# Second attention reordered with its attended product in halves, expert requests reordered, unread products in the waits of the router: one change to a two-layer trunk with experts

## What is computed

```python
def neighborhood_attention(h_lat, h_ctx, w_qkv, w_o, rpb, ctx_out):      # layer 1, 16 heads of 64
    ...
    s_loc = einsum(q_r, k_blk) + bias                                    # bias is -1e30 outside the window
    s_ctx = einsum(q_r, kc)
    p = softmax(concatenate([s_loc, s_ctx], -1))
    o = einsum(p[..., :n_loc], v_blk) + einsum(p[..., n_loc:], vc)
    ...
    return o @ w_o

def moe_ffn(h, router_w, router_bias, w_gate, w_up, w_down):
    scores = sigmoid(h @ router_w); sel = scores + router_bias
    # the best of 4 groups, the best 2 experts in it; gates from their scores
    for e in range(16):
        y = y + gates[:, e:e+1] * ((silu(h @ w_gate[e]) * (h @ w_up[e])) @ w_down[e])
```

## Time and profile before

| what | value |
|---|---|
| median of 3 runs | 1212.77 us (1210.61 to 1214.37) |
| the profiled execution | 1215.52 us |
| its span, first to last instruction | 1213.4 us |
| mean granted TensorE clock | 0.905 |
| PE, DVE, ACT, POOL busy | 79%, 33%, 31%, 18% of the span |
| layer 0: router and experts | about 405 to 676 us |
| attention of layer 1 | about 828 to 907 us |
| layer 1: router and experts | about 942 to 1185 us |

### The profile page before, as it was taken

One profiled execution on the slowest core, in us unless ns is written; L12 is line 12 of the kernel. 1 busy time (PEld: TensorE's weight loads), 2 busy tenths in 40 slices (PEclk: granted clock), 3 DMA queues, 4 the chain that ended last, 5 costly groups with the idle time before them and its releaser, 6 DMA issues.

```text
span 1213.4 us, 24157 instructions
## 1 busy us (share of the span) xinstructions
PE 957.7 (79%) x9458; PEld 638.5 (53%) x9459; DVE 402.5 (33%) x809; ACT 372.5 (31%) x803; POOL 218.3 (18%) x329
## 2 busy tenths in 40 slices
PE   3699999978799488897998389997889279876540
PEld 0477776535455344564766268885445147653320
DVE  1433330557623512121221562224543612221103
ACT  3533222557511222121222453235432112221102
POOL 0000000000000044343443105700000233442211
PEclk8899999999899689898999789999889589998875
DMA  9766655996401839999997574317037769999972
GB/s 342 255 230 230 213 208 208 319 388 233 194 14 44 338 108 413 422 422 425 422 423 298 185 199 114 139 60 287 1 89 302 286 260 420 421 423 423 425 323 110
DMA packets 93681, 322.05 MB, mean 265 GB/s; under 512 B 21241, under 2 KB 33954, under 8 KB 81330
## 3 DMA queue, kind: packets, MB, share of 16 engines
q1 hardware_dynamic: 85746, 305.40, 65.1%
q0 software_dynamic: 7008, 12.62, 2.8%
q10 hardware_dynamic: 864, 3.15, 0.6%
HBM read 313.67 MB, written 13.99 MB: 270 GB/s over the span
## 4 chain that ended last, share of the span: by engine, by line
PE 58%; DMA 24%; DVE 8%; SPq 4%; issue 3%; ACT 3%; POOL 1%; DVEq 0%; POOLq 0%; ACTq 0%
PE ps L1641 20%; PE ps L1859 19%; DMA expert_sets<-in_moe_w_up_dram 17%; PE ps L1783 7%; PE ps L1544 3%; DMA ada_late<-in_ada_w_dram 3%; PE ps L1568 2%; PE ps L1747 2%; DMA ring<-in_diff_w_qkv_dram 2%; SPq L608 1%; PE ps L1694 1%; SPq L590 1%; DMA expert_rows<-moe,scatter_idx 1%; DVE att L1312 1%; DMA val<-expert_rows 1%
## 5 line engine op out<-in xcount | busy, mean ns | idle before, releaser
L1859 PE MATMUL ps<-expert_sets,moe 128*32 128x256 f32 x6304 | 370.2, 397 | 98.5 <-DMA expert_sets<-in_moe_w_up_dram 67.8
L1859 PEld LDWEIGHTS ps<-expert_sets,moe 128*32 128x32 f32 x6304 | 243.2, 115 | 224.1 <-issue 123.4
L1502 DVE STREAM_TRANSPOSE moe<-moe 128x256 f32<-128x256 f32 x70 | 45.9, 655 | 326.9 <-PE ps L1859 305.7
L1641 PE MATMUL ps<-w_high,x_high 128*128 128x512 f32 x352 | 141.8, 403 | 6.1 <-DVE hT L506 2.7
L1641 PE MATMUL ps<-w_high,x_low 128*128 128x512 f32 x352 | 138.9, 394 | 0.0
L1641 PE MATMUL ps<-w_low,x_high 128*128 128x512 f32 x352 | 138.4, 393 | 0.0
L1066 ACT ACTIVATE moe<-ps 128x128 f32<-128x128 f32 x68 | 18.9, 278 | 273.8 <-PE ps L1859 271.6
L741 POOL MEMSET moe<- 128x128 f32 x2 | 0.4, 204 | 566.4 <-PE ps L1809 566.4
L473 DVE TENSOR_TENSOR w_low<-ring,w_high 128x2048 fp32r<-128x2048 f32 x24 | 56.5, 2359 | 131.6 <-ACT w_high L470 131.6
L764 POOL DMA_INDIRECT expert_rows<-moe,scatter_idx x74 | 75.9, 1025 | 78.5 <-POOL scatter_idx L801 57.9
L1641 PEld LDWEIGHTS ps<-w_high,x_high 128*128 128x128 f32 x352 | 66.9, 190 | 30.1 <-issue 17.1
(11 more groups left out here) (233 smaller groups left out, 1066.4 us busy)
## 6 DMA issues: line engine op xcount, KB each, us to landing
expert_sets<-in_moe_w_down_dram SPq DMA_DIRECT2D x32, 2048.0 KB, 24.2
expert_sets<-in_moe_w_gate_dram SPq DMA_DIRECT2D x30, 2048.0 KB, 22.2
expert_sets<-in_moe_w_up_dram SPq DMA_DIRECT2D x30, 2048.0 KB, 27.3
ring<-in_ada_w_dram SPq DMA_DIRECT2D x16, 2048.0 KB, 8.1
ring<-in_diff_w_qkv_dram SPq DMA_DIRECT2D x6, 2048.0 KB, 8.2
ada_late<-in_ada_w_dram SPq DMA_DIRECT2D x6, 2048.0 KB, 11.7
ring<-in_na_w_qkv_dram SPq DMA_DIRECT2D x6, 2048.0 KB, 9.6
rows<-mod_rows SPq DMA_DIRECT2D x12, 512.0 KB, 8.6
```

The lines of the kernel that those rows point to most:

```text
L1502: dve.transpose(blk_inT, blk_in[b].rearrange("p (j k) -> p k j", k=KC)).then_inc(m_xt[l], 1)
L1641: mm = pe.matmul(ps[:, n % 2], x_part[:, k, tok], w_part, start=(k == 0 and i == 0), stop=(k == KC - 1 and i == 2))
L1859: mm = pe.matmul(ps[g * SLOTS:(g + 1) * SLOTS, bank, 0:n_out], lhs_T[:, k, :], weights(k, g), start=(k == 0), stop=(k == n_chunks - 1), sk ...
```

## The change

Three things change. In the attention of layer 1, PE's loop goes by pairs of units: scores of u and u+1 first, then the turn of u-3, then half of an attended product (two of the four key tiles; the sums are spread ahead of the first half), then the turn of u-2; ahead of each turn of an even unit stands one product 128*128 by 256 whose result nobody reads, between the wait for the bank and the wait for the exponentials. DVE's `scale_out(g)` moves to behind the maximum of unit 4g+11, ahead of the inversion there. In the experts' requests, gate and up of position 4 are requested ahead of the down part of position 3. And PE makes 19, 9 and 11 (layer 0) or 13, 7 and 10 (layer 1) unread products of 128*128 by 256 into bank 3 in the three waits of the router.

```diff
@@ load_experts
+                later_parts(l, EXTRA + 1, (gate_set(EXTRA + 1), None), (0, 1), back=4)
                 later_parts(l, EXTRA, (None, EXTRA % 3), (2,))
-                for p in range(4, 7):
+                later_parts(l, EXTRA + 1, (None, (EXTRA + 1) % 3), (2,))
+                for p in range(5, 7):
                     later_parts(l, p, (gate_set(p), p % 3), (0, 1, 2), back=4)
@@ DVE, attention of layer 1
+                        if u % 4 == 3 and u >= 11:
+                            scale_out(u // 4 - 2)
                         if u % 2 == 1 and 3 <= u < U + 3:
                             invert_sums(u - 3)
-                        if u % 4 == 0 and u >= 8:
-                            scale_out(u // 4 - 2)
@@ PE, turn_probs1(u)
-                        pe.wait_ge(s_ex[1], u + 1)
                         if u >= 2:
                             pe.wait_ge(s_pc[1], u - 1)
+                        if u % 2 == 0:
+                            pe.matmul(ps[:, (4, 7)[u % 2], 0:2 * P], ident, cst[:, 0:2 * P], start=True, stop=True)
+                        pe.wait_ge(s_ex[1], u + 1)
@@ PE, attend1(g) becomes broadcast_sums(g), with the waits for s_oe and s_rc and the four small products, and
+                    def attend1(g, keys):
+
                         pe.wait_ge(s_pc[1], 4 * g + 4)
-                        for k in range(TILES):
+                        for k in keys:
...
-                        mm.then_inc(s_pv[1], 1)
+                        if keys[-1] == TILES - 1:
+                            mm.then_inc(s_pv[1], 1)
@@ PE, the loop
-                    for u in range(U + 4):
-                        if u < U and u % 2 == 0:
+                    for u in range(0, U + 8, 2):
+                        if u < U:
                             scores1(u)
+                        if 3 <= u < U + 3:
+                            turn_probs1(u - 3)
+                        if u >= 8 and u % 4 == 0:
+                            broadcast_sums(u // 4 - 2)
+                            attend1(u // 4 - 2, (0, 1))
+                        if u >= 8 and u % 4 == 2:
+                            attend1(u // 4 - 2, (2, 3))
                         if 2 <= u < U + 2:
                             turn_probs1(u - 2)
-                        if u % 4 == 3 and u >= 7:
-                            attend1(u // 4 - 1)
@@ PE, router
+                def keep_busy(count):
+
+                    for _ in range(count):
+                        pe.matmul(ps[:, 3, 0:2 * P], ident, cst[:, 0:2 * P], start=True, stop=True)
+
+                keep_busy((19, 13)[l])
                 pe.wait_ge(s_set, l + 2)
                 pe.wait_ge(s_ch[l], 1)
...
+                keep_busy((9, 7)[l])
                 pe.wait_ge(s_oh[l], 2)
...
                 mm.then_inc(s_tab[l], 1)
+                keep_busy((11, 10)[l])
```

More of the change, by code:

```diff
@@ L1731, in turn_probs1, with broadcast_sums @@
                         mm.then_inc(s_pt[1], 1)
-                    def attend1(g):
+                    def broadcast_sums(g):
                         if g >= 2:
```

## The result

The changed kernel took **1195.96 us** (median of 4 runs, 1195.34 to 1196.78) against 1211.69 (1206.1 to 1214.37) of the kernel before on the same chip: a ratio of 0.9877 (95% interval 0.984 to 0.9913), 15 us faster by the ratio and 15.7 by the medians. The forecast was 1180.1 with a range of 1173 to 1194. So the direction was right, about half of the gain came, and the time lies outside the range. The profiled execution took 1196.78 us, its span is 1194.7. The profiled execution of the kernel before took 1215.52, so the two traces lie 18.7 us apart, 3 more than the medians.

A forecast was written before the change was run, and what follows sets the result against it. Order of the program and clock were taken to bound the attention, weights the experts, with idle DMA ahead of them. Savings 17.7 + 6.0 + 6.5 + 0.5 + 2.0 = 32.7 us turn the median 1212.8 into 1180.1; range 1173 to 1194.

The forecast's parts named there:

- Part 1, the attention: Attention of layer 1: PE never waits and sets the pace, 79.5 us become 61.8, 17.7 saved if the clock stays full.
- the price of the pieces: Attention of layer 1: PE's pieces at full clock sum to 51.8 us for 32 units, plus 7.0 for unread products.
- filling and end: Attention of layer 1: 1.8 us of wait stay while filling, and 1.2 at the end before the output products.
- the unread products are paid in full: Attention of layer 1: exponentials come in time, so 16 unread products cost 7.0 us, except three in the filling.
- Part 2, layer 0: Layer 0's experts: weights requested 6.9 us earlier, 6.0 gained after a bit of PE's own work.
- Rival B: First experts: PE stalls there, or its own work holds layer 0, taking most of its 6.0 us: 1185; chance 0.12.
- Part 2, layer 1: Layer 1's experts: first weight request 6.5 us earlier, queues stay full, all 6.5 us gained.
- Part 3: Router: unread products in PE's waits hold the clock, gaining 0.5 us in layer 0 and 2.0 in layer 1.
- a faster first block: Layer 1's first expert block, nearly all at half clock before: between 0 and 3.1 us gained, 1.0 taken.
- theory S: Missing 16 us: sizes of the attention's pieces and its unread products that were never hidden explain most.
- I: Missing 16 us: PE stops for instructions at places set by code length; fetches come late while weights fill the queues.
- R: Rival for the missing 16 us: the router's products stall PE or cost time at half clock; no chance given.

The follow-up runs named there:

- run 4: The changed kernel without the 16 unread products in the attention: 1187.39 us, ratio 0.9802 to the kernel before.
- Run 6: The changed kernel with the old order of weight requests in both layers: 1202.86 us, ratio 0.9913 to the kernel before.
- run 2: The kernel before with only the early request of gate and up of position 4: 1203.75 us, ratio 0.9927.
- run 7: The changed kernel with the early request in layer 0 alone: 1196.96 us, ratio 0.9879 to the kernel before.
- run 12: The changed kernel without the router's unread products, the attention's kept: 1197.13 us, ratio 0.9899 to the kernel before.
- run 8: The changed kernel without the attention's unread products, with 9 instead of 19 ahead of layer 0's ranks and 18 instead of 10 behind layer 1's table: 1186.85 us.
- run 1: The kernel before with the new attention of layer 1 alone, its 16 unread products included: 1200.66 us, ratio 0.9911.
- run 5: The changed kernel with later-requested weight parts moving only 64 columns of each row, leaving out most weight traffic: 1100.86 us (one run).

## Why the prediction was half right

**Part 1, the attention: 17.7 forecast, 14.8 measured** (79.44 to 64.65). The mechanism held point by point: pairs every 3.72 and 4.16 us, no idle time in the turns, clock 1.00 all through, DVE and ACT at 42.7 and 42.5 us under it, no wait for the modulation rows. The term that was mis-sized is the price of the pieces, taken from stretches of one kind: 8 groups at 7.88 instead of 7.36 are 4.2 more, while filling and end took about 1.6 instead of 3.0. And one step, though priced right, should have led further: "the unread products are paid in full". I charged 7.0 us for something the order didn't need; run 4 measured 6.8 in the stage (8.6 in all), at an unchanged clock.

**Part 2, layer 0: 6.0 forecast, about 6 measured.** Run 6 against the change gives 4.4 to 6.9 us in the whole kernel; run 2 alone ends the layer 6.2 earlier. Over all traces with full weights its experts end at 672.3 to 677.1 without the early request and at 668.3 to 673.1 with it, 5.3 earlier in the mean. PE's stops grew from 5.5 to 9.4 us there and waits for weights fell from 18.7 to 7.2. Rival B's mechanism was present in layer 0, but the weights' waits had room for it.

**Part 2, layer 1: 6.5 forecast, nothing measured** (run 7 against the change, and the table of pairs). This is the step that failed: "From there on the queues stay full up to the last weights, at one rate, so the whole train of loads moves forward by that, as long as PE, which frees the buffers, moves with it." The condition didn't hold. PE lost its own progress to instruction fetches: stops of 2 to 5 us, 13.9 in sum for 8.1. Since only freed buffers can be asked for, the queues ran nearly dry from 1005 to 1015, until the request at 1014.42. Rival B named this mechanism and looked for it in layer 0; it was layer 1, whose first four positions have one block each and so a jump at every one, that paid. The one stop of 4.47 at 990.26 in the earlier trace rows was the warning: it was read as a single event and not as a price that every jump under full queues may have. The same trace had another in the middle of a block, 2.71 us in front of 1042.64, which the rows didn't take in. The Trainium skill, "Runtime: NRT & Kernel Launch", Instruction fetch mechanics, has both halves: a taken branch out of the window waits for a DMA, and the crossing of a block boundary in straight code is mostly hidden. The trace agrees with the second outside the experts (25 packets, no stop). In the experts it agrees with the first, and shows more: with the weights early PE stands also 17 matmuls behind a jump, 2.76 us for 0.28 to 0.55.

**Part 3: 2.5 forecast, 1 to 3 measured** (run 12). The size came out, not the way. In layer 0 the clock stayed at half from about 405 to some 412, so 19 products took 11.1 us (406.38 to 417.51), not the 9.4 assumed. The ranks are 4.8 late, of which 1.6 stems from an earlier stage of this execution, and 3.2 is the products' own. Ranks and table gave it back in part. In layer 1 the first block was hardly shorter (5.85 us for 6.50): the clock had fallen in the 5.01 idle before it, as feared. Whether a full clock there arrives at the end is open: of the traces with full weights the four whose first block ran at full clock (3.66 us) need 213.3 to 216.7 us from it to the end of the experts, the nine others 215.5 to 220.3. Which of the two, the clock or the stops, holds back each microsecond isn't separated further.

**The sum, followed along the span** (after against before; the forecast in brackets): end of layer 0's experts 5.6 us earlier [6.5], first scores of layer 1 4.8 [6.5], first output product 19.6 [24.2], first block of layer 1 20.7 [25.2], end of its experts 19.1 [32.7]. Of the 13.6 us missing at the end, some 2 are in and behind layer 0, 2.9 in the attention, none in the router of layer 1 and 9 from its first block on: the 6.5 of the step that failed, the 1.0 of a faster first block, and 1.6 given back. So theory S accounts for 3 of them, I for most of the rest, and R for nothing that stands clear of the intervals. By the medians 16 us are missing, since the trace of the kernel before is of a slower execution than the median.

**A better version.** The change without the attention's unread products (run 4: 1187.39 us, ratio 0.9802), or run 8 (1186.85, 0.9787), beats both kernels; the two can't be told apart.

## What to carry to other kernels

When an order is found in which the engine never waits, products made to hold its clock may not be needed, and they are paid in full, so try the order without them first. Price short pieces from stretches in which kinds alternate, not from runs of one kind. Before a stream of transfers is started earlier, ask what else uses the DMA engines: in a long program with jumps the instructions come over them too, and come later once the stream is on. The work that frees the stream's buffers then runs later.

## What the runs showed of the hardware that I had not expected

- PE stops in the middle of a block of the experts, 17 to 46 matmuls behind a jump, at a place that moves with the number of instructions ahead of it (177, 187, 198, 202, 206 matmuls into layer 1's experts). The stop is 0.28 to 0.55 us in runs 1, 5, 6 and 7, where the 16 KB instruction packet lands ahead of PE, and 1.5 to 3.4 in the runs with the weights early, where it lands with PE's arrival or behind it.
- In code written out in a line 25 such packets, 16 us and more apart, landed with no stop of PE, one of them in 4 us with full DMA engines.
- Where a loop turns back PE stands 0.9 to 1.3 us, with light traffic or full queues and with no instruction packet near. At a jump with a packet it stood up to 3.1 us with light traffic and 1.3 to 6.5 with the full weights. In sum the stops cost 5.4 and 7.4 us in the two layers with light weights, and 5 to 16.5 us a layer in the other runs.
- Where one kind of short float32 product follows another on PE about 0.1 us is added: 1.02 for a half product of 0.92, 0.53 for an unread one of 0.44.
- The granted clock stayed at 1.00 for 58 us of alternating scores, turns and attended products at 95% busy, with turns in 32 places and no filler.
- At the router of layer 0 in the changed kernel the clock, at 0.50 from about 405, stayed there through some 6 us of unread products without a gap.
